# The head of a four-FFN decoder trunk: three first weight tiles multiplied together, chunk pair by chunk pair

## The reference

```python
def rmsnorm(x, g):
    xf = x.astype(jnp.float32)
    y = xf * lax.rsqrt(jnp.mean(xf * xf, axis=-1, keepdims=True) + EPS)
    return (y * g.astype(jnp.float32)).astype(x.dtype)
def swiglu(h, w_gate, w_up, w_down):
    return (jax.nn.silu(h @ w_gate) * (h @ w_up)) @ w_down
...
    for i in range(DEPTH):
        h = rmsnorm(x, ln_gains[i, 0])
        x = x + 0.5 * swiglu(h, ffn_w_gate[i, 0], ffn_w_up[i, 0], ffn_w_down[i, 0])
        h = rmsnorm(x, ln_gains[i, 1])
```

## Time and profile before

| | |
|---|---|
| median of 3 runs | 876.4 us (876.39 to 876.97) |
| the profiled execution, its own time | 878.0 us |
| its span on the core | 876.0 us |
| PE busy | 866.6 us, 99% of the span |
| DVE busy | 642.9 us, 73% |
| ACT busy | 463.2 us, 53% |
| DMA | 159.68 MB, 182 GB/s on average |

### The profile page before, as it was taken

How to read it: one execution, slowest core, us unless ns; L and a number is a source line. 1 busy time by engine, 2 the same in 40 slices (tenths; PEclk the granted TensorE clock), 3 DMA queues, 4 the chain that set the end, 5 groups by cost and what they waited for, 6 DMA issues and landing times.

```text
span 876.0 us, 12479 instructions
## 1 busy us (share of the span) xinstructions
PE 866.6 (99%) x5234; PEld 763.4 (87%) x5234; DVE 642.9 (73%) x742; ACT 463.2 (53%) x536; POOL 22.7 (3%) x49
## 2 busy tenths in 40 slices
PE   8999999999999999999999999999999999999997
PEld 7888888889999988888888888888888988888886
DVE  6998776568776699777656697777656998777452
ACT  6665555345555666555534375555544675555441
POOL 1000005300000000000000000000000000000000
PEclk9999999999999999999999999999999999999999
DMA  8677555565434447555455556555565277565431
GB/s 285 197 249 231 191 176 174 181 201 180 149 144 146 144 137 247 193 191 182 164 196 187 185 187 200 191 192 181 170 196 175 97 241 234 184 213 186 146 119 48
DMA packets 154166, 159.68 MB, mean 182 GB/s; under 512 B 2888, under 2 KB 152448, under 8 KB 154112
## 3 DMA queue, kind: packets, MB, share of 16 engines
q1 hardware_dynamic: 153760, 158.35, 55.5%
q10 hardware_dynamic: 352, 0.55, 0.2%
HBM read 157.84 MB, written 1.05 MB: 181 GB/s over the span
## 4 chain that ended last, share of the span: by engine, by line
PE 98%; DMA 1%; DVE 0%; SPq 0%; ACT 0%; issue 0%; DVEq 0%; ACTq 0%
PE psum L430 97%; DMA band<-in_x_dram 1%; PE psum L744 1%; PE psum L727 1%; PE psum L460 0%; PE psum L618 0%; ACT soft L917 0%; SPq L366 0%; SPq L364 0%; DVE band L1184 0%; DVE scratch L1227 0%; DVE scratch L1196 0%; DVEq L75 0%; DVE mean L1208 0%; DVE rstd L1091 0%
## 5 line engine op out<-in xcount | busy, mean ns | idle before, releaser
L430 PE MATMUL psum<-xg,w_hi 128*128 128x512 f32 (+1 forms) x1664 | 490.1, 379 | 0.1
L1046 DVE TENSOR_TENSOR w_lo<-raw,w_hi 128x2048 fp32r<-128x2048 f32 (+1 forms) x149 | 332.3, 2232 | 109.8 <-ACT w_hi L825 109.8
L430 PEld LDWEIGHTS psum<-xg,w_lo 128*128 128x128 f32 x1536 | 289.0, 188 | 62.5
L825 ACT ACTIVATE w_hi<-raw 128x2048 fp32r<-128x2048 f32 (+1 forms) x150 | 279.5, 1867 | 112.5 <-PE psum L430 112.0
L430 PE MATMUL psum<-xg,w_lo 128*128 128x256 f32 x1536 | 312.8, 278 | 0.0
L430 PEld LDWEIGHTS psum<-xg,w_hi 128*128 128x128 f32 x1664 | 254.4, 189 | 1.8 <-issue 0.9
L430 PE MATMUL psum<-h_all,w_hi 128*128 128x512 f32 (+1 forms) x656 | 189.4, 374 | 0.0
L430 PEld LDWEIGHTS psum<-h_all,w_lo 128*128 128x128 f32 x592 | 111.4, 188 | 23.4
L430 PE MATMUL psum<-h_all,w_lo 128*128 128x256 f32 x592 | 121.8, 278 | 0.0
L430 PEld LDWEIGHTS psum<-h_all,w_hi 128*128 128x128 f32 x656 | 100.2, 189 | 0.8 <-issue 0.8
L859 ACT ACTIVATE scratch<-psum 128x512 f32<-128x512 f32 x44 | 26.1, 594 | 80.8 <-PE psum L430 80.8
(11 more groups left out here) (114 smaller groups left out, 477.5 us busy)
## 6 DMA issues: line engine op xcount, KB each, us to landing
raw<-in_ffn_w_up_dram SPq DMA_DIRECT2D x43, 1024.0 KB, 5.1
raw<-in_ffn_w_gate_dram SPq DMA_DIRECT2D x42, 1024.0 KB, 5.1
raw<-in_ffn_w_down_dram SPq DMA_DIRECT2D x24, 1024.0 KB, 5.2
raw<-in_attn_w_qkv_dram SPq DMA_DIRECT2D x12, 1024.0 KB, 5.2
raw<-in_ffn_w_down_dram SPq DMA_DIRECT2D x20, 512.0 KB, 4.4
raw<-in_ffn_w_down_dram SPq DMA_DIRECT2D x12, 768.0 KB, 4.4
raw<-in_attn_w_o_dram SPq DMA_DIRECT2D x4, 1024.0 KB, 4.9
band<-in_x_dram SPq DMA_DIRECT2D x4, 256.0 KB, 5.2
```

The lines of the kernel that those rows point to most:

```text
L430: return nc.tensor.matmul(out, stationary, moving, start=start, stop=stop, skip_group_check=True)
L825: nc.scalar.activation(w_hi[:, n % SPL, 0:size], raw[:, n % RAW, 0:size], ACT.Copy).then_inc(hi_split, 1)
L1046: nc.vector.tensor_tensor(w_lo[:, n % SPL, 0:size], raw[:, n % RAW, 0:size], w_hi[:, n % SPL, 0:size].bitcast(f32), ALU.subtract).then_inc ...
```

## The change

Tiles 0, 1 and 2 (`FIRST = 3`) are multiplied together. x and the three tiles come in five steps: chunk 0, chunk 1, then pairs of chunks (`STEPS`); tiles 1 and 2 come in four pairs (`PAIRS`), from step 1 on. In each step SP issues x first and then a piece of each tile, 18 loads in place of 12. PE multiplies the step's chunks with tile 0, then tile 1, then tile 2, into six PSUM banks (0 to 5); x is transposed into the two others by turns, three pieces of tiles ahead of its use, and therefore DVE must copy x out of PSUM at once (`x_acc`, `x_done`), in copies of one chunk. From step 2 on, ACT and DVE split the piece of tile 0 ahead of the step's x. Tile 3, which shares its slot with tile 0, comes in two halves; its second lo half stands between mean and reciprocal. The wait for the load of tile 3 is unchanged in kind (the last lo split of tile 0). There are 13 idle transposes in place of 16. ACT's list (not shown) has the same order as DVE's: splits of the pieces of tile 0, 1, 2 of a step, with x behind the piece of tile 0, `square_x` behind each step from the third on, and tile 3 in halves.

```diff
-    HALVED = 2
+    FIRST = 3
+    STEPS = ((0,), (1,), (2, 3), (4, 5), (6, 7))
+    PAIRS = ((0, 1), (2, 3), (4, 5), (6, 7))
...
+    def first_pieces(n):
+        return STEPS if n == 0 else PAIRS
+    def step_of(k):
+        return [s for s, ks in enumerate(STEPS) if k in ks][0]
+    def step_tiles(s):
+        return [(n, s if n == 0 else s - 1) for n in range(FIRST) if n == 0 or s]
...
+        def x_acc(d):
+            s = step_of(d)
+            at = STEPS[s].index(d) * SEQ
+            return psum[:, 6 + s % 2, at:at + SEQ]
...
-                        if n > HALVED:
+                        if n > FIRST:
                             load(n, cols, src[:, :, group])
...
+                        elif n == FIRST:
+                            sp.wait_ge(lo_split, n - RAW + 1)
                             for half in range(2):
                                 ks = slice(half * DC // 2, (half + 1) * DC // 2)
-                                sp.dma_start(cols(raw[:, n, :])[:, ks, :], src[:, ks, group]) \
-                                  .then_inc(raw_loaded[n] if half else half_loaded[n - 1], 16)
-                    if n == HALVED + 1:
-                        sp.dma_start(late_rows[0:DC, :], pool_scale[0].rearrange("(c p) -> c p", p=P)) \
-                          .then_inc(late_loaded, 16)
+                                sp.dma_start(cols(raw[:, n % RAW, :])[:, ks, :], src[:, ks, group]) \
+                                  .then_inc(raw_loaded[n % RAW] if half else half_loaded, 16)
...
-            for c in range(DB):
-                pair = slice(c * GW, (c + 1) * GW)
-                sp.dma_start(x_tok[:, :, pair], x_v[:, :, pair]).then_inc(x_loaded[c], 16)
-                ks = slice(2 * c, 2 * c + 2)
-                sp.dma_start(cols(raw[:, 0, :])[:, ks, :], gate_v[0, 0][:, ks, 0:GW]) \
-                  .then_inc(piece_loaded[c] if c < DB - 1 else raw_loaded[0], 16)
+            first_src = (gate_v[0, 0][:, :, 0:GW], up_v[0, 0][:, :, 0:GW], gate_v[0, 0][:, :, GW:2 * GW])
+            for s, chunks in enumerate(STEPS):
+                x_cols = slice(chunks[0] * P, (chunks[-1] + 1) * P)
+                sp.dma_start(x_tok[:, :, x_cols], x_v[:, :, x_cols]).then_inc(x_loaded[s], 16)
+                for n, i in step_tiles(s):
+                    piece = first_pieces(n)[i]
+                    ks = slice(piece[0], piece[-1] + 1)
+                    sp.dma_start(cols(raw[:, n, :])[:, ks, :], first_src[n][:, ks, :]) \
+                      .then_inc(raw_loaded[n] if i == len(first_pieces(n)) - 1 else first_loaded[n][i], 16)
+            sp.dma_start(late_rows[0:DC, :], pool_scale[0].rearrange("(c p) -> c p", p=P)).then_inc(late_loaded, 16)
...
-                        if j == 0 and side == 0:
-                            if norm == 0 and k in (1, 3):
-                                x_transposes(k // 2 + 2)
+                        if j == 0 and side == 0 or n < FIRST:
                             pe.wait_ge(xg_lo_done, norm * DC + k + 1)
-                        if n == FFN0:
-                            if k < DC - 2:
-                                pe.wait_ge(piece_lo, k // 2 + 1)
-                            else:
-                                pe.wait_ge(lo_split, 1)
-                        elif n <= HALVED and k == 0:
-                            pe.wait_ge(half_lo, n)
+                        if n == FIRST and k == 0:
+                            pe.wait_ge(half_lo, 1)
...
                 if f == 0:
-                    column_chunks(0, 0, range(DC))
-                    column_chunks(0, 1, range(DC))
-
-                    pe.wait_ge(x_done, DC // 2)
-                    column_chunks(1, 0, range(DC // 2))
-                    pe.wait_ge(x_done, DC)
-                    statistics(norm)
-                    pe.wait_ge(late_loaded, 16)
-                    nc.tensor.transpose(psum[:, stats_bank(0), SEQ:SEQ + DC], late_rows[:, :],
-                                        ident[0:DC, 0:DC]).then_inc(late_T, 1)
-                    column_chunks(1, 0, range(DC // 2, DC))
-                    weights(n0 + 3)
+                    for s in range(len(STEPS)):
+                        for n, i in step_tiles(s):
+                            piece = first_pieces(n)[i]
+                            if n == 2 and s == len(STEPS) - 1:
+                                pe.wait_ge(x_done, DC)
+                                statistics(norm)
+                                pe.wait_ge(late_loaded, 16)
+                                nc.tensor.transpose(psum[:, stats_bank(0), SEQ:SEQ + DC], late_rows[:, :],
+                                                    ident[0:DC, 0:DC]).then_inc(late_T, 1)
+                            if i < len(first_pieces(n)) - 1:
+                                pe.wait_ge(first_lo[n], i + 1)
+                            else:
+                                weights(n)
+                            column_chunks(n // 2, n % 2, piece[0:1])
+                            if n == 0 and 0 < s < len(STEPS) - 1:
+                                x_transposes(s + 1)
+                            column_chunks(n // 2, n % 2, piece[1:])
...
-            def x_transposes(c):
-                pe.wait_ge(x_loaded[c], 16)
-                for d in (2 * c, 2 * c + 1):
+            def x_transposes(s):
+                pe.wait_ge(x_loaded[s], 16)
+                if s > 1:
+                    pe.wait_ge(x_done, STEPS[s - 2][-1] + 1)
+                for d in STEPS[s]:
                     for t in range(TT):
-                        last = nc.tensor.transpose(y_acc(d)[:, t * P:(t + 1) * P], x_tok[:, t, d * P:(d + 1) * P],
+                        last = nc.tensor.transpose(x_acc(d)[:, t * P:(t + 1) * P], x_tok[:, t, d * P:(d + 1) * P],
                                                    ident[:, :])
-                last.then_inc(x_T if c < DB - 1 else x_T_last, 1)
+                last.then_inc(x_T, 1)
...
-            idle_transposes(8)
+            idle_transposes(7)
...
-            idle_transposes(6)
+            idle_transposes(2)
             x_transposes(1)
-            idle_transposes(2)
+            idle_transposes(4)
...
+            def inverse_mean(norm, cols=slice(0, SEQ), between=None):
                 dve.wait_ge(stats_done, norm + 1)
                 newton_step(nc.vector.tensor_scalar(mean[:, cols], psum[:, stats_bank(norm), cols], 1.0 / D, EPS,
                                                     ALU.mult, ALU.add))
+                if between:
+                    between()
...
+            for s, chunks in enumerate(STEPS):
+                if s < 2:
+                    for d in chunks:
+                        rest_chunk(0, d)
+                for n, i in step_tiles(s):
+                    final = i == len(first_pieces(n)) - 1
+                    if final:
+                        dve.wait_ge(hi_split, n + 1)
+                    else:
+                        dve.wait_ge(first_hi[n], i + 1)
+                    piece = slice(first_pieces(n)[i][0] * GW, (first_pieces(n)[i][-1] + 1) * GW)
+                    nc.vector.tensor_tensor(w_lo[:, n, piece], raw[:, n, piece], w_hi[:, n, piece].bitcast(f32),
+                                            ALU.subtract).then_inc(lo_split if final else first_lo[n], 1)
+                    if n == 0:
+                        if s == len(STEPS) - 1:
+                            add_squares(0, 1)
+                        if s > 1:
+                            for d in chunks:
+                                rest_chunk(0, d)
+                        for d in chunks:
+                            nc.vector.tensor_copy(x[:, d, :], x_acc(d)).then_inc(x_done, 1)
             add_squares(0, 2)
             add_squares(0, 3)
             fold_squares(0)
-            split_lo_half(2, 1)
-            split_lo(3)
+            def split_lo_half(half):
+                if half:
+                    dve.wait_ge(hi_split, FIRST + 1)
+                else:
+                    dve.wait_ge(half_hi, 1)
+                part = slice(half * ROWS // 2, (half + 1) * ROWS // 2)
+                nc.vector.tensor_tensor(w_lo[:, FIRST, part], raw[:, FIRST % RAW, part],
+                                        w_hi[:, FIRST, part].bitcast(f32),
+                                        ALU.subtract).then_inc(lo_split if half else half_lo, 1)
+            split_lo_half(0)
             dve.wait_ge(late_T, 1)
             nc.vector.tensor_copy(gains[:, NORM_ROWS:NORM_ROWS + DC], psum[:, stats_bank(0), SEQ:SEQ + DC]).then_inc(gains_done, 1)
-            inverse_mean(0)
+            inverse_mean(0, between=lambda: split_lo_half(1))
```

More of the change, by code:

```diff
@@ L292, in wait_pair @@
         def wait_pair(eng, norm, c):
[L293 to L298 removed]
+            if norm == 2:
                 if c < DB - 1:
@@ L488, in column_chunks @@
                                                 xg[:, k], k == 0, k == DC - 1) for m in range(GM)])
-                    if k == DC - 1:
```

(50 more changed lines are left out.)

65 lines of the change are left out of this document (22 added, 43 removed).

## The result

The changed kernel takes 878.29 us in the median of 21 runs (877.98 to 879.11). The kernel before, run beside it on the same chip, takes 876.98 us (876.36 to 878.75, 21 runs), 0.6 us above the median of three runs from which the forecast started. The ratio is 1.0014, with a 95% interval of 1.0007 to 1.002: slower by 1.2 us (0.6 to 1.8; the medians are 1.3 apart), and within the 0.2% that the forecast called no change. The forecast was 876.9, with a range up to 878.1, 0.2 us short of what was measured.

A forecast was written before the change was run, and what follows sets the result against it. PE, busy 866.6 of 876.0 us, bounds the kernel; its head ends with DVE's split of tile 5. Statistics +0.54 and tile 5's chain -0.06 sum to +0.5 us: median 876.4 to 876.9, range 875.4 to 878.1.

The forecast's parts named there:

- The mechanism: Head: PE still waits for the third x load, then about 1.26 us at tile 5 for DVE's split.
- the sign: Whole kernel: slower by +0.5 us, with tile 5 at 39.0 in place of 38.53.
- the sum: Head to tile 5: +0.54 - 0.06 = +0.5 us; profiled execution 878.0 to 878.5, median 876.4 to 876.9.
- Step 1: Head, third x load: issued at 3.83, 5.2 us on its way, lands at 9.0; 9.19 before.
- Step 2: Third x landing to statistics: 15.32 us of PE work plus 0.04 for the semaphore; statistics at 24.36, 0.54 later.
- Step 3: Statistics to PE's start of tile 5: 14.65 us, 0.06 sooner than before, PE waiting about 1.26 for DVE's split.
- The clock: Rival, PE in the head: idling drops its clock, three products cost +2.1, sum +2.6, 879 us; chance 0.06.
- The expectation: Recorded before rerunning the changed kernel: 878.3 us and little spread, since tile 5 waits for DVE's chain.

The follow-up runs named there:

- experiment 3: Changed kernel with ACT's and DVE's splits of tile 5 moved earlier; 876.85 us against 877.07 for the kernel before, ratio 0.9995.
- experiment 1: The kernel before, run again unchanged and profiled a second time; median 876.91 us against 877.07, ratio 0.9997; profiled 876.82 us.

## Why the prediction missed

The mechanism was right, the sign was right, and each term for the changed kernel came within 0.5 us; the start of the sum was wrong.

- **Step 1 (landing).** Forecast 9.0, found 8.84 and 8.53. The issue is at 3.77 instead of 3.83, and 5.07 and 4.77 us on the way instead of 5.2.
- **Step 2 (landing to statistics).** Forecast 15.36, found 15.39: 20 products and three transpositions behind the restart, without a wait of over 0.1 us, as summed. DVE's fold ended at 23.61, 0.6 us ahead of PE, where the forecast had 0.9 of cover.
- **Step 3 (statistics to tile 5).** Forecast 14.65, found 14.70, with a wait of 1.26 forecast and 1.22 found. Two small errors in it cancel: the reciprocal begins 2.45 us behind the statistics and not 2.33, and PE takes the tile 0.06 us behind the split, where the sum had 0.11 and the earlier trace rows have 0.13. DVE's split set it, through the reciprocal behind tile 3's second half, and experiment 3 shows what the wait costs.
- **The profiled execution.** Forecast 878.5, found 878.55. That is partly luck: the second profile took 878.23.
- **The clock.** PE did not fall back: its row at 8.88 takes 0.66 us for four transposes, as at 9.23 before. The rival did not occur; what did is that the first product, at 5.98, still ran at the slow rate, which cost nothing, since PE waited for x behind it.

The step that failed is the side of *before* in step 1, "9.19 before", and with it the last line of the sum, where the +0.5 us worked out against the profiled execution (878.0) was added to the median (876.4). The forecast took the 1.6 us between these two as an offset that both kernels share. It was not: the load was 6.37 us on its way in that one execution, and 5.21 and 5.3 in the two later profiles. So a usual landing of the changed kernel was set against a late one of before. With 5.2 us for both, before lands at 2.82 + 5.2 = 8.02, where experiment 1 found it, its statistics are at 22.65, the new ones at 24.36, and the sum is 1.71 - 0.06 = +1.65 us: 878.05 from the median of 876.4. That 5.2 fits both kernels is luck: it is the median of only four x loads of the late execution, which took 3.2, 4.1, 6.4 and 6.8 us, and the four of the second profile have 4.7. With what was found the difference is +0.51 for the landing (8.53 against 8.02), +0.76 in step 2 (15.35 against 14.59), -0.01 in step 3 and +0.09 behind tile 5: +1.35 us, where the medians are 1.3 apart. Of the 1.4 us by which the median was missed, 0.6 lies in the median of three runs, 876.4 where 21 gave 876.98, and 0.8 in this sum.

The plain runs fit: four of the 21 runs of before lie at 878.06 to 878.75, about where the first profile was, and most of the rest near 877.0. Of all 102 runs of before beside these kernels, 20 took 878.0 us or more. That these are late loads was not measured, since plain runs leave no trace. The changed kernel has no such group: its runs span 1.1 and 0.7 us, against 2.4 for before. The expectation put that down to the chain of DVE at tile 5, but this chain begins at the statistics and would be shifted with them, so why it is so is open.

The hint was in the forecast itself: it said that the profiled execution took 1.6 us more than the median. In the traces, 2 us lie between span and time, in each kernel, so an excess has a place in the span. No row of that one profile said where: the 6.37 us stand beside the 6.8 of the next x load. Only a second profile shows it.

Why the earlier third x load gives little in the median, the three profiles with that edit show in part: it leaves the chain, and what takes its place, the first piece of tile 1 or PE's own slow start, varies from execution to execution. PE's product behind the third transposition begins at 8.35, 8.69 and 9.00 in them, and at 8.86 to 9.30 in the four profiles of the changed kernel and its variants without the edit. Open remains how often each occurs, and why the loads were late in the first profile.

## What to carry to other kernels

When the profiled execution is slower than the median of plain runs, take a second profile before summing, and compare the landings of the loads in the two; both kernels must be priced with executions of the same kind. Work moved ahead of a point from which another engine's chain starts doesn't shorten the time if that chain, and not the engine itself, sets the end: two products moved ahead of the statistics came back as a wait for DVE at tile 5. Then start that engine's next piece earlier, which here took the whole wait away.

## What the runs showed of the hardware

The same 256 KB load, issued at the same time, landed at 9.19 in one execution of before and at 8.02 in another, with nothing changed, together with the load ahead of it, and the whole kernel was shifted by 1.2 us. The Trainium skill (DMA: Bandwidth & Descriptors, Anatomy of one DMA) prices a DMA that GpSimd issues at about 2.0 us plus its bytes at 436 GB/s, 2.6 us for 256 KB, an estimate from that page. These loads are issued by SP, with others ahead of them, and took 5.21 and 6.37 us, so the rows decide.

The moment at which PE's instructions get faster at the start also moves. In the changed kernel the first product takes 1.31 us and the second 0.71. The stretches of each, and of the products behind the restart. The columns are the stretch and its length; busy time and instructions of PE, its weight loads, DVE, ACT and POOL; PE's granted clock; the busy share of the DMA engines; GB/s:

```profile
5.98:7.29 1.31, 1.31 (x7) 1.12 (x6) 1.31 (x5) 0.77 (x2) 0.00 (x0) 1.00 0.85 265
7.29:8.00 0.71, 0.71 (x6) 0.56 (x4) 0.42 (x1) 0.57 (x1) 0.00 (x0) 1.00 0.90 309
8.88:24.20 15.32, 15.32 (x92) 13.53 (x93) 13.02 (x26) 11.74 (x22) 0.00 (x0) 1.00 0.77 252
```

The granted clock reads 1.00 in all three, so the slow start does not show in that column, and is read from durations alone. They differ by about two, like the levels of 1.2 and 2.4 GHz, and PE had worked since 1.58 when the rate rose. In the control with tile 5's split earlier in before, six transposes take 1.49 us at 4.68, where the earlier trace rows has 0.91 at 4.93:

```profile
4.68 1.49 PE L626 MATMUL psum<-ident 128*128 128x128 f32 x6
6.42 1.12 PE L618 MATMUL psum<-ident,band 128*128 128x128 f32 x4 [0.24 <-DMA band<-in_x_dram]
...
22.57 0.60 PE L430 MATMUL psum<-sq_sum,ones 128*128 128x256 f32 x2
```

With this start the first product comes at 7.61 and not at 6.80, as in before, again, and PE is at the third pair of x only at 8.44; it no longer waits for that load, which landed at 7.78. Yet the statistics of this execution are the earliest of all, at 22.57. From 8.44 on PE goes through in 14.13 us in place of 14.59: the slow start used up waits that PE would have had for loads and splits.
